# Lookup stage: four more u tiles ahead of the wait for the indices, the first coefficients weighted at the tail's end, 16 late dots moved into the V stage

## What is computed

```python
q = (xb @ wq).reshape(blk, PEER_HEADS, 2, PEER_DK)
s = jnp.einsum('nhpd,hpkd->nhpk', q, keys)
s1, i1 = lax.top_k(s[:, :, 0], PEER_TOPK)
s2, i2 = lax.top_k(s[:, :, 1], PEER_TOPK)
...
sc, pos = lax.top_k(cand, PEER_TOPK)
idx = jnp.take_along_axis(cidx, pos, axis=-1)
g = jax.nn.softmax(sc.astype(jnp.float32), axis=-1)
act = jax.nn.gelu(jnp.einsum('nhkd,nd->nhk', u_tab[idx], xb), approximate=False)
return jnp.einsum('nhk,nhkd->nd', (g * act).astype(v_tab.dtype), v_tab[idx])
```

## Time and profile before

| | us |
|---|---|
| median of 3 runs (5565.71 to 5578.42) | 5570.98 |
| the profiled execution | 5567.87 |
| its span, first to last instruction | 5566.2 |
| PE busy | 5256.6 (94%) |
| DVE busy | 3513.3 (63%) |
| ACT busy | 1824.7 (33%) |
| POOL busy | 841.8 (15%) |
| granted TensorE clock, mean | 0.973 |

### The profile page before, as it was taken

One profiled execution on the slowest core, in us unless ns is written; L12 is line 12 of the kernel. 1 busy time (PEld: TensorE's weight loads), 2 busy tenths in 40 slices (PEclk: granted clock), 3 DMA queues, 4 the chain that ended last, 5 costly groups with the idle time before them and its releaser, 6 DMA issues. The chain is left out here.

```text
span 5566.2 us, 85344 instructions
## 1 busy us (share of the span) xinstructions
PE 5256.6 (94%) x31278; PEld 4877.7 (88%) x31278; DVE 3513.3 (63%) x6925; ACT 1824.7 (33%) x2772; POOL 841.8 (15%) x646
## 2 busy tenths in 40 slices
PE   8999999898999998999889999998989999989998
PEld 6777877898998998999867778778989989989998
DVE  2543544333899886888634435443338998868886
ACT  2322222322333563333223222223223335633332
POOL 0000000000122113433200000000001221134442
PEclk9999999999999999999999999999999999999999
DMA  3222221222687999999722222212226879999997
GB/s 118 54 72 68 55 71 40 85 80 103 214 270 227 303 323 361 379 354 354 273 101 66 60 67 55 72 40 85 85 98 216 271 227 303 324 359 380 354 354 271
DMA packets 513982, 1056.59 MB, mean 190 GB/s; under 512 B 93012, under 2 KB 306004, under 8 KB 511828
## 3 DMA queue, kind: packets, MB, share of 16 engines
q1 hardware_dynamic: 421508, 716.84, 38.5%
q0 software_dynamic: 92160, 335.59, 16.6%
HBM read 909.80 MB, written 144.77 MB: 189 GB/s over the span
## 5 line engine op out<-in xcount | busy, mean ns | idle before, releaser
L1705 PE MATMUL ps<-parts,splits 128*128 128x416 f32 (+1 forms) x7488 | 1383.1, 344 | 40.5 <-ACT go L2078 25.6
L1705 PEld LDWEIGHTS ps<-parts,splits 128*128 128x128 f32 x7488 | 1328.4, 189 | 53.8 <-issue 30.2
L2420 PE MATMUL ps<-parts,splits 128*128 128x416 f32 x6144 | 1163.1, 352 | 21.3 <-DVEq L2475 17.2
L2420 PEld LDWEIGHTS ps<-parts,splits 128*128 128x128 f32 x6144 | 1154.5, 189 | 29.9 <-DVEq L2475 17.9
L168 PE MATMUL ps<-xn,wr 128*128 128x288 f32 x1952 | 495.7, 409 | 13.1 <-PEq L108 10.7
L168 PEld LDWEIGHTS ps<-xn,wr 128*128 128x128 f32 x1952 | 364.0, 190 | 126.2 <-issue 33.7
L1454 PE MATMUL ps<-parts,wmh 128*128 128x288 f32 x2048 | 414.2, 298 | 27.5 <-DVE parts L1512 27.5
L1760 POOL IOTA iota<- 128x128 f32 x2 | 0.5, 230 | 2789.7 <-POOLq L108 2789.7
L2121 DVE TENSOR_TENSOR splits<-raw,splits 128x1024 fp32r<-128x1024 f32 x288 | 352.7, 1225 | 63.3 <-ACT splits L2003 57.8
L1454 PEld LDWEIGHTS ps<-parts,wmh 128*128 128x128 f32 x2048 | 330.7, 190 | 29.1 <-issue 29.1
L2003 ACT CAST splits<-raw 128x1024 fp32r<-128x1024 f32 x288 | 304.3, 1057 | 8.0 <-DVE second L2116 4.4
(11 more groups left out here) (439 smaller groups left out, 8577.5 us busy)
## 6 DMA issues: line engine op xcount, KB each, us to landing
raw<-in_u SPq DMA_DIRECT2D x256, 512.0 KB
raw<-in_v SPq DMA_DIRECT2D x128, 512.0 KB
more<-in_v SPq DMA_DIRECT2D x128, 512.0 KB
wr<-in_w_cm SPq DMA_DIRECT2D x104, 512.0 KB, 4.4
activated<-go SPq DMA_DIRECT2D x256, 208.0 KB, 1.9
coefficients<-wt SPq DMA_DIRECT2D x26, 2048.0 KB
first<-activated SPq DMA_DIRECT2D x32, 832.0 KB, 7.0
wb<-coefficients SPq DMA_DIRECT2D x32, 832.0 KB
```

The source lines that it names most:

```text
L1705: last = nc.tensor.matmul(out, wp[:, slot, k, :], xp[:, k, cols], start=(k == 0 and wp is T.wh and xp is T.xh), stop=(k == KD - 1 and wp i ...
L2420: last = nc.tensor.matmul(out, vp[:, r % 4, m * P:(m + 1) * P], coef, start=(r == 0 and vp is T.vh and gp is T.xh), stop=(ends and vp is T ...
```

## The change

- U_STATIC is 68 in place of 64, so 84 tiles stand before the transposes and 8 in the tail. SP spreads the last head's indices inside its loop (at tile 81).
- ACT takes the softmax's Exp after the Gelu of tile 81 (TILES_STATIC - 3) instead of tile 78 (TILES_STATIC - 2). DVE does `low` of one tile while Exp runs and four after the weights are found.
- Folded columns lie in the order of the heads, the early ones at 128 to 143, the late ones at 144 to 159. The weights' copies are four in place of eight.
- The tail has 12 late dots (columns 116 to 127), two a tile. Its first coefficients are multiplied at t = 6 of 8 and split after the last tile.
- The 16 late folded dots (LATE_FOLDS) are done in the V stage: in tiles 0 to 63, POOL gathers a u slot into T.gf[1] after plain gather 4i + 2, DVE takes the dot after blend 4i + 1. All folded v slots of that time go through T.gf[0] alone. After tile 63 ACT takes the Gelu of the late columns and DVE the weights; from then on both T.gf are used in turn again.

```diff
-U_STATIC = 8 * PH_HEADS
+U_STATIC = 8 * PH_HEADS + WRING
...
-TAIL_DOTS = SLOTS + FSLOTS - EARLY_DOTS - BEAT_DOTS
+TAIL_DOTS = SLOTS - LATE_FIRST
+FOLD_LATE = SLOTS + EARLY_HEADS * FTOP
+LATE_FOLDS = SLOTS + FSLOTS - FOLD_LATE
...
-    return SLOTS + (FTOP * h + FSLOTS // 2) % FSLOTS
+    return SLOTS + FTOP * h
...
-            spread(PH_HEADS - 1)
             sp.wait_ge(s["found"], 1)
...
-                if n == TILES_STATIC - 2:
+                if n == TILES_STATIC - 3:
                     act.wait_ge(s["exp_in"], 1)
                     nc.scalar.activation(T.t2[:], T.t2[:], ACT.Exp).then_inc(s["exped"], 1)
...
+            lows(n, 1)
             dve.wait_ge(s["exped"], 1)
...
-            lows(n, 1)
+            lows(n + 1, WRING)
             for z in range(3):
...
-                for j, c in tail[3 * t:3 * t + 3]:
+                for j, c in tail[2 * t:2 * t + 2]:
...
-                if t == 4:
+                if t == U_TAIL - 2:
                     dve.wait_ge(s["early_g"], 16)
                     dve.wait_ge(s["early_w"], 16)
...
-                if j % FOLD == 0:
-                    i = j // FOLD
-                    if i >= 2:
+                i = j // FOLD
+                if i < LATE_FOLDS:
+                    if j % FOLD == 0:
+                        if i:
+                            pool.wait_ge(s["folded"], i)
+                        gather_rows(nc, T, table, SLOTS + i, T.gf[0]).then_inc(folds_in[0], 16)
+                    if j % FOLD == 2:
+                        if i:
+                            pool.wait_ge(s["dotted"], i)
+                        gather_rows(nc, T, T.d["u_rows"], FOLD_LATE + i, T.gf[1]).then_inc(folds_in[1], 16)
+                elif j % FOLD == 0:
+                    if i > LATE_FOLDS:
                         pool.wait_ge(s["folded"], i - 1)
+                    else:
+                        pool.wait_ge(s["folded"], i)
+                        pool.wait_ge(s["dotted"], i)
                     gather_rows(nc, T, table, SLOTS + i, T.gf[i % 2]).then_inc(folds_in[i % 2], 16)
...
-            with act.Fori(1, BLOCKS - 1) as p:
+            with act.Fori(1, LATE_FOLDS // 2) as p:
+                steps(p, False, False)
+            act.wait_ge(s["dotted"], LATE_FOLDS)
+            late = T.gact[:, FOLD_LATE:]
+            nc.scalar.activation(late, late, ACT.Gelu).then_inc(s["gated"], 1)
+            with act.Fori(LATE_FOLDS // 2, BLOCKS - 1) as p:
                 steps(p, False, False)
...
+            def dot_folded(p, i):
+                dve.wait_ge(folds_in[1], 32 * p + 16 * i + 16)
+                nc.vector.scalar_tensor_tensor(
+                    out=T.gf[1], in0=T.gf[1], scalar=1.0, in1=T.xrow_f, op0=ALU.mult, op1=ALU.mult,
+                    accum_out=T.gact[:, bass.ds(FOLD_LATE + 2 * p + i, 1)]).then_inc(s["dotted"], 1)
...
                     blend(p, x, first)
+                    if dots and x % FOLD == 1:
+                        dot_folded(p, x // FOLD)
                     if x % FOLD == FOLD - 1:
-                        blend_folded(p, x // FOLD, first)
...
+                        blend_folded(p, x // FOLD, first, dots)
...
+            dve.wait_ge(s["gated"], 1)
+            late = slice(FOLD_LATE, SLOTS + FSLOTS)
+            nc.vector.tensor_tensor(T.gact[:, late], T.gact[:, late], T.gw[:, late], ALU.mult).then_inc(s["shared"], 1)
```

More of the change, by code:

```diff
@@ L1723, in late_columns @@
 def late_columns():
-    yield from range(LATE_FIRST, FOLD_LATE)
+    yield from range(LATE_FIRST, SLOTS)
 def gather_rows(nc, T, table, j, out):
@@ L1825, in _ @@
             for f in range(FOLD):
[L1826 to L1829, removed]
+                sp.dma_start(T.gw[f * NF:(f + 1) * NF, SLOTS:].rearrange("p (h k) -> p h k", h=PH_HEADS),
+                             shares[:, :, f, :]).then_inc(s["shares"], 16)
             def beats(cc, last):
@@ L2072, in _ @@
                     act.wait_ge(s["dotted"], EARLY_DOTS + BEAT_DOTS)
-                    for soon in (T.gact[:, 0:LATE_FIRST], T.gact[:, FOLD_LATE:]):
+                    for soon in (T.gact[:, 0:LATE_FIRST], T.gact[:, SLOTS:FOLD_LATE]):
                         last = nc.scalar.activation(soon, soon, ACT.Gelu)
@@ L2082, in _ @@
                                    ).then_inc(s["a_high"], 1)
-            act.wait_ge(s["dotted"], SLOTS + FSLOTS)
-            late = T.gact[:, LATE_FIRST:FOLD_LATE]
+            act.wait_ge(s["dotted"], EARLY_DOTS + BEAT_DOTS + TAIL_DOTS)
+            late = T.gact[:, LATE_FIRST:SLOTS]
             nc.scalar.activation(late, late, ACT.Gelu).then_inc(s["gated"], 1)
@@ L2351, in value_stage @@
     with stage(nc, "h_in", "h_out", "w0", "w1", "g0", "g1", "v0", "v1", "v2", "v3", "v4", "v5", "v6", "v7", "weighed", "a_high",
-               "a_low", "v_high", "v_low", "v_used", "u0", "u1", "u2", "u3", "f0", "f1", "blended", "folded", "chosen", "finished", "joined", "evicted",
+               "a_low", "v_high", "v_low", "v_used", "u0", "u1", "u2", "u3", "f0", "f1", "blended", "folded", "dotted", "gated", "shared", "chosen", "finished", "joined", "evicted",
                shared=T.bridge, closing=T.bridge) as (block, s):
@@ L2498, in blend, with blend_folded @@
                                                    in1=T.acc, op0=ALU.mult, op1=ALU.add).then_inc(s["blended"], 1)
-            def blend_folded(p, i, first):
-                dve.wait_ge(folds_in[i], 16 * p + 16)
+            def dot_folded(p, i):
[3 more added lines that the diff above has]
+                    accum_out=T.gact[:, bass.ds(FOLD_LATE + 2 * p + i, 1)]).then_inc(s["dotted"], 1)
+            def blend_folded(p, i, first, dots):
+                b = 0 if dots else i
+                dve.wait_ge(folds_in[b], 32 * p + 16 * i + 16 if dots else 16 * p + 8 * LATE_FOLDS + 16)
                 share = T.gact[:, bass.ds(SLOTS + 2 * p + i, 1)]
                 if first and i == 0:
-                    nc.vector.tensor_scalar(T.acc_f, T.gf[i], share, None, ALU.mult).then_inc(s["folded"], 1)
+                    nc.vector.tensor_scalar(T.acc_f, T.gf[b], share, None, ALU.mult).then_inc(s["folded"], 1)
                 else:
                     dve.wait_ge(s["folded"], 2 * p + i)
-                    nc.vector.scalar_tensor_tensor(out=T.acc_f, in0=T.gf[i], scalar=share, in1=T.acc_f,
+                    nc.vector.scalar_tensor_tensor(out=T.acc_f, in0=T.gf[b], scalar=share, in1=T.acc_f,
                                                    op0=ALU.mult, op1=ALU.add).then_inc(s["folded"], 1)
@@ L2511, in _, with steps @@
                 a_low(0, x)
-            def steps(p, first, last):
+            def steps(p, first, last, dots):
                 for x in range(BLOCK):
@@ L2535, in _ @@
                                         ).then_inc(s["chosen"], 1)
-            with dve.Fori(1, BLOCKS - 1) as p:
-                steps(p, False, False)
-            steps(BLOCKS - 1, False, True)
+            with dve.Fori(1, LATE_FOLDS // 2) as p:
+                steps(p, False, False, True)
+            dve.wait_ge(s["gated"], 1)
+            late = slice(FOLD_LATE, SLOTS + FSLOTS)
+            nc.vector.tensor_tensor(T.gact[:, late], T.gact[:, late], T.gw[:, late], ALU.mult).then_inc(s["shared"], 1)
+            dve.wait_ge(s["shared"], 1)
+            with dve.Fori(LATE_FOLDS // 2, BLOCKS - 1) as p:
+                steps(p, False, False, False)
+            steps(BLOCKS - 1, False, True, False)
             dve.wait_ge(s["h_in"], 16)
@@ L2677, in program @@
                 T.xrow = sb(peer, "xrow", [P, D])[:]
+                T.xrow_f = sb(peer, "xrow_f", [P, D])[:]
                 T.gidx = sb(peer, "gidx", [P, SLOTS + FSLOTS], U32)[:]
```

23 lines of the change are left out of this document (10 added, 13 removed).

## The result

| | before | after |
|---|---|---|
| median, us (4 runs each) | 5569.28 (5565.71 to 5578.42) | 5813.39 (5811.17 to 5817.46) |
| profiled span, us | 5566.2 | 5811.1 |
| granted TensorE clock, mean | 0.973 | 0.959 |

What follows compares the result with a forecast made beforehand. TensorE was taken as the bound, its standing still as what can be won. Per layer a V-stage loss of 60 us less lookup gains of 5.9 and 11.7, twice, is +85: 5656 us, range 5565 to 5740.

Steps and rivals of the forecast that it cites:

- Part 1: Lookup, four more u tiles before the indices: wait of 7.0 us falls to 1.9, gain 5.9 us a layer.
- Part 2: Lookup's tail shortened to 8 tiles and 12 dots: wait 12.9 to 7.8 us, gain 11.7 us a layer.
- Part 3: 16 dots in the V stage: POOL's wait for the folded blend closes a loop, loss 60 us a layer.
- The DVE term: V stage loop: after the dot's rows land, DVE needs 8.1 us to the end of the next folded blend.
- group 0: First group of four V-stage tiles: its folded blend ends 28.7 us after the stage's start S.
- Group 1: Second group of V-stage tiles, in the backlog: takes 25.7 us, ending 54.4 us after the stage's start S.
- I take 13.9: V stage: chosen landing of the dot's rows after POOL's burst starts, between 9.9 and 17.6 us, giving a 22.0 us loop.
- the upper bound of 17.6: V stage: latest landing of the dot's rows, from a full queue: 8.3 us for the first gather, 3.1 for each later.
- the lower bound: V stage: earliest landing of the dot's rows, 9.9 us: 6.0 for a gather alone, issued three times 1.3 us later.
- rival B: V stage loop worse: above 24.5 us, POOL's issues stretched to 4.7 us; 5758 us at a loop of 25.7; chance 8%.
- T: Length of the V stage's closed loop per group of four tiles: 18.0 to 25.7 us, taken as 22.0, against 18.1 for products.
- A: V stage: dot's rows land within 10 us of the burst, loop hides, gains stand: 5546 us, faster; chance 15%.

Runs made afterwards that it cites:

- dots_in_tail: The changed kernel with all 28 late dots left in the tail, four a tile, and the V stage of before: 5580.4 us, ratio to before 1.0019.
- before_with_wait: The kernel before, with only the wait of folded gathers 2 to 16 made stricter (folded blend i-1, not i-2), no dots moved: 5676.8 us, 1.0194.
- late_fold: The changed kernel with the folded gather and its wait behind row 4i+3 instead of row 4i in tiles 0 to 63: 5529.8 us, ratio to before 0.9939.
- third_buffer: The changed kernel with a third buffer for the dots, so folded gathers keep two and wait as before: 5536.6 us, ratio to before 0.9939.
- short_coefficients: The changed kernel with the V stage's loads of wb cut to one chunk of 13: 5765.4 us.
- short_v: The changed kernel with the V stage's loads of v cut to 128 of 1024 columns: 5728.5 us.
- dot_second: The changed kernel with the dot's gather issued right behind the folded one, ahead of rows 4i+1 and 4i+2: 5774.1 us.
- dot_ahead: The changed kernel with the dot's gather issued ahead of the folded gather's wait: 5685.4 us.

## Why the prediction was wrong in size

**Part 1** held. Forecast: a wait of 1.9 us and a gain of 5.9; measured 2.16, and the products behind the two short gaps take 4.79 and 4.72 us where one took 6.21, at a granted clock of 1.00 (4722 to 4727 us) where it was 0.75 (4595 to 4602 in before). So the short gaps cost no clock; I had counted half of that.

**Part 2** held: 7.65 us for 7.8, an end of 3.08 us (gap) for some 4.0, tail 48.9 us for 49.2. The slow last product took 6.33 us for 5.5, and the shorter end made up for it. dots_in_tail shows the dots' part in it.

**Part 3, mechanism: right.** POOL waits for the folded blend once a group (16.3 us; some 13 forecast), then issues in a row; DVE waits for row 4i+1 and the dot, TensorE for DVE's parts, the second half runs through (TensorE's last wait of the kind ends at 5523.26). before_with_wait, late_fold and third_buffer show that the loop over that one wait is the cause. The DVE term was right: 8.0 us for 8.1. So was group 0: its folded blend ends at S + 29.4 (5095.31 - 5065.93), forecast S + 28.7. Group 1, the backlog's, was already too short at 25.7: 28.2 us, to S + 57.6. And the lower clock was hidden, as said: 96 matmuls took 19.5 to 20.8 us in place of 18.1, and TensorE still waited 4.2 to 9.4 us behind each such group, where some 4 were forecast.

**Part 3, the step that failed: "I take 13.9"**, the landing of the dot's rows behind the folded blend. It is 20.5 us in the turn shown and 27.4 - 8.0 = 19.4 in the mean; it lies above the upper bound of 17.6 too. Some 15 turns x (27.4 - 22.0) x 2 layers = 162 us, and 5656 + 162 = 5818 against 5813: the whole miss, as near as this sum goes. Three parts of it were mis-sized:

- The issues. I put the dot's 3.9 us behind the burst's start for the lower bound. It went out 8.8 us after (5341.60 to 5350.42), since the first two took 3.52 and 2.53 us, in all turns of the closed loop but the second. That turn shows the price, 3.8 us of the group (27.7 - 23.9), and its landing of 15.9 us lies within my bounds. The sentence on 4.7 us stretched issues, taken as rival B and priced at some 3 us of T, was the common case. The Trainium skill (SBUF — State Buffer, SBUF: two separate sides) has the mechanism, and the trace agrees in kind: the 3.52 us issue starts within DVE's weighing and lies under it and what DVE does next, and those behind 5348, when DVE stands still, take 0.99.
- What stands beside it. I took the mean of 76% of full as a reason to go to the middle of the bounds. But this closed loop packs its transfers: 6.3 MB moved in 16 us at 0.4 MB per us, next to 11 us with little or none, 4.6 of them right behind the folded blend. The landing then depends on the bytes in the burst, SP's included, as short_coefficients and short_v show, and not on the mean share.
- The order. I let one gather land every 3.1 us in the order of issue. The counts above show that the later ones share with it. The rule that I cited beside the upper end, turns between two queues (DMA: Bandwidth & Descriptors, Queues, rings and completion order, in the Trainium skill), made it come down, to 23.9. The trace agrees with the half: POOL's queue has 1.59 of 3.24 MB from 5352 to 5360, and 2.95 of 6.25 MB from 5346 to the landing. But my sum counts four gathers, where nearly six have moved.

Of the 5.5 us (19.4 - 13.9) the long issues are thus the largest part seen, some 3.5 to 4 us. How the rest divides between the other two stays open; what the runs give is the dot's place in the burst 1.3 us, wb's 0.77 MB 1.4, v's 1.8 MB 2.6, the dot and its gather altogether 4.7 (27.4 to 22.7). No kernel was built without the long issues, so their size rests on that one turn.

**Rivals.** A (the loop fits, 5546) is what late_fold and third_buffer made true, at 5530 and 5537; not by a faster landing, but by the wait's slack. B, "the loop is worse", was the right one, long issues included, at 27.4 us above its 25.7 and at 8% far too unlikely. The lower end for the landing came from a gather alone, the upper from gathers issued 1.3 to 2.8 us apart at the V stage's start; neither begins with an issue of 3.5 us.

## What to carry to other kernels

When a change takes away a buffer, look at what stands behind the new wait on that engine's queue, and at what releases it: if the released work ends in the same release, it is a closed loop and its length counts, not the mean load. In such a loop size a landing by all bytes that the release sets free, on every queue, plus the time in which nothing moves; mean bandwidth says little. Look too at what the other engine does when the released instruction is issued: here the same gather took 0.99 or 3.52 us to issue, by whether it began ahead of DVE's weighing or within it. The cure is in the order: put the instruction that waits longest behind those that the loop needs first; here one moved gather turned 4.4% slower into 0.6% faster, with no work taken away.

## What was not expected of the hardware

- An indirect gather's issue on POOL takes 0.99 us with DVE idle, and 3.50 to 3.52 us when it starts some 0.9 us into DVE's weighing (1.89 us), with a split (1.22 us) right behind, the next one 2.53; after, dot_second, short_coefficients, short_v, dot_ahead and before_with_wait all show these numbers. Started 0.21 us ahead of the weighing it takes 0.99, and the next 1.68 (after, 5124.40).
- Six gathers in flight, issued over 12 us, are nearly all moved when the fourth lands (2.95 and 3.05 of 3.1 MB). While both POOL's queue and SP's had work, from 5352 to 5360, they moved nearly the same bytes (1.59 and 1.64 MB).
- A gap of 1.6 us left the next product at 4.72 us; after gaps of 4.2 to 9.4 us the granted clock was 0.5 for a time, the lower of its two levels (1.2 GHz), and 96 matmuls took 19.5 to 20.8 us. Two windows of after, the gap ahead of 5365.17 and the products behind it (busy times as above, PEclk, DMA share, GB/s):

```profile
5362.00:5366.00 4.00, 0.83 (x2) 0.83 (x3) 3.85 (x5) 0.00 (x0) 0.00 (x0) 0.50 0.25 77
5366.00:5370.00 4.00, 4.00 (x13) 3.82 (x12) 4.00 (x5) 0.00 (x0) 0.00 (x0) 0.50 0.38 123
```
